# A first projection in three rounded passes, its norm factor moved to the outputs

## The reference, cut to what matters

```python
h = rms_norm(x, g_mix)          # x * rsqrt(mean(x*x) + eps) * g_mix
proj = h @ w_in                 # 2048 -> 4176 + 3360 columns
p_dsa, p_rwkv = proj[..., :DSA_COLS], proj[..., DSA_COLS:]
q, k, v, q_idx, k_idx, w_idx = split_cols(p_dsa, DSA_SPLITS)
y_dsa = dsa_mixer(...)          # indexer picks keys, then softmax attention
p_rwkv = token_shift_mix(p_rwkv, rwkv_shift_mix)   # mixes each token with the one before
y_rwkv = rwkv7_mixer(...)       # a recurrence over tokens, 16 heads of 64
x = x + concat([y_dsa, y_rwkv]) @ w_out
```

## Time and profile before

| | us |
|---|---|
| median of 3 runs | 3308.83 |
| lowest to highest | 3307.78 to 3310.36 |
| the profiled execution's own time | 3304.67 |
| its span, first to last instruction | 3302.9 |
| TensorE busy | 3166.9 (96%) |
| weight loads busy | 2718.0 (82%) |
| VectorE busy | 1857.9 (56%) |
| ScalarE busy | 1396.1 (42%) |
| GpSimd busy | 211.2 (6%) |

### The profile page before, as it was taken

How to read it: one execution, slowest core, us unless ns; L and a number is a source line. 1 busy time by engine, 2 the same in 40 slices (tenths; PEclk the granted TensorE clock), 3 DMA queues, 4 the chain that set the end, 5 groups by cost and what they waited for, 6 DMA issues and landing times.

```text
span 3302.9 us, 46085 instructions
## 1 busy us (share of the span) xinstructions
PE 3166.9 (96%) x18702; PEld 2718.0 (82%) x18702; DVE 1857.9 (56%) x2416; ACT 1396.1 (42%) x1951; POOL 211.2 (6%) x263
## 2 busy tenths in 40 slices
PE   8999999998989999999898899999999999999998
PEld 7777777766768888767797779999998989889896
DVE  3433333356577777767656883444565555545454
ACT  2222222244456666656541013665434434434343
POOL 0000000020000000000137630000000000000000
PEclk9999999998989999999999998999999999999999
DMA  6222222221358888778553333444555555555554
GB/s 239 83 77 77 90 77 79 88 77 67 115 210 325 318 324 315 286 284 308 190 190 119 124 114 123 166 164 178 208 191 179 204 191 185 186 189 183 189 184 148
DMA packets 81782, 581.66 MB, mean 176 GB/s; under 512 B 9009, under 2 KB 9265, under 8 KB 12338
## 3 DMA queue, kind: packets, MB, share of 16 engines
q1 hardware_dynamic: 78912, 566.27, 47.3%
q10 hardware_dynamic: 2674, 12.54, 1.0%
HBM read 574.58 MB, written 4.19 MB: 175 GB/s over the span
## 4 chain that ended last, share of the span: by engine, by line
PE 80%; DVE 11%; DMA 3%; ACT 2%; POOL 2%; issue 1%; SPq 0%; ACTq 0%; DVEq 0%; POOLq 0%
PE PG L784 10%; PE PG L724 8%; PE PG L722 8%; PE PG L725 8%; PE PG L750 5%; PE PG L749 5%; PE PG L748 5%; PE PG L1103 3%; PE PG L1104 3%; PE PG L1105 3%; PE PX L854 3%; DMA ring<-weights 3%; DVE work L2344 2%; DVE ring_r L612 2%; PE PG L693 1%
## 5 line engine op out<-in xcount | busy, mean ns | idle before, releaser
L612 DVE TENSOR_TENSOR ring_r<-ring,work_r 128x1024 fp32r<-128x1024 f32 x532 | 629.9, 1225 | 394.7 <-ACT work_r L605 389.7
L605 ACT ACTIVATE work_r<-ring 128x1024 fp32r<-128x1024 f32 x532 | 534.4, 1052 | 577.5 <-PE PG L725 235.1
L784 PE MATMUL PG<-HT,ring 128*128 128x256 f32 x1728 | 435.1, 389 | 0.0
L612 DVE TENSOR_TENSOR ring_r<-ring,C_r 128x1024 fp32r<-128x1024 f32 x244 | 289.2, 1226 | 222.2 <-ACT C_r L605 218.9
L605 ACT ACTIVATE C_r<-ring 128x1024 fp32r<-128x1024 f32 x244 | 244.9, 1052 | 374.7 <-PE PG L725 255.6
L725 PE MATMUL PG<-work_r,ring_r 128*128 128x256 f32 x1344 | 374.8, 279 | 0.0
L725 PE MATMUL PG<-YT_r,ring_r 128*128 128x256 f32 x1280 | 361.2, 282 | 0.0
L784 PEld LDWEIGHTS PG<-HT,ring 128*128 128x128 f32 x1728 | 311.2, 190 | 55.4 <-issue 10.6
L725 PEld LDWEIGHTS PG<-work_r,ring_r 128*128 128x128 f32 x1344 | 253.3, 188 | 0.0
L749 PE MATMUL PG<-ring_r,HT_r 128*128 128x512 f32 x640 | 252.1, 394 | 0.0
L725 PEld LDWEIGHTS PG<-YT_r,ring_r 128*128 128x128 f32 x1280 | 244.5, 191 | 0.0
(11 more groups left out here) (566 smaller groups left out, 6277.0 us busy)
## 6 DMA issues: line engine op xcount, KB each, us to landing
ring<-weights SPq DMA_DIRECT2D x536, 1024.0 KB, 4.8
XT<-xT SPq DMA_DIRECT2D x4, 512.0 KB, 6.1
XT<-x ACTq DMA_DIRECT2D x1, 2048.0 KB, 9.4
residual<-XT ACTq DMA_DIRECT2D x4, 512.0 KB, 3.0
XT<-residual ACTq DMA_DIRECT2D x1, 2048.0 KB, 10.1
result<-YT SPq DMA_DIRECT2D x8, 256.0 KB, 4.1
C<-constants ACTq DMA_DIRECT2D x1, 1608.0 KB, 9.3
work<-gate_up ACTq DMA_DIRECT2D x1, 1024.0 KB, 13.0
```

Of the source, the lines that this page charges most:

```text
L605: act.activation(w_high(u)[:, c], ring[:, u % RING, c], ACT.Copy).then_inc(w_hi, 1)
L612: dve.tensor_tensor(ring_r[:, u % RING, c], ring[:, u % RING, c], w_high(u)[:, c].bitcast(F32), ALU.subtract).then_inc(w_lo, 1)
L784: mm = pe.matmul(PG[:, u % BANKS, 0:T], ring[:, u % RING, k * P:k * P + P], HT[:, k, :], start=(k == 0), stop=(k == KT - 1))
```

## The change

The first projection is computed in three passes too. Its weights are rounded by half units: `half_high(act, h)` on ScalarE writes half h (0 to 119) into one of four places, and `half_low(eng, h)` subtracts in place, on VectorE for halves 0 to 15 and on GpSimd for the others. `product(u, k)` waits for its half's low part and issues three matmuls. Two halves of one unit are released separately (`half_done`, `unit_done`).

The norm's factor is no longer in the inputs. The inputs are x times `g_mix`, rounded (`HT_r`) and the rest (`XT_r`), so that products can start before the mean square is known. The factor `RS` is applied to the outputs: on r, k, v and misc by VectorE as it takes them from PSUM (`with_factor`), after which ScalarE and VectorE mix them in SBUF; on the first 25 dsa tiles by GpSimd; on the value tiles by ScalarE when it writes them as tokens, with `RS` turned to columns.

In the rounds, ScalarE's halves and VectorE's and GpSimd's further duties are put between the steps by `used_halves`, by the step in which the half four before has been used. "lora" of the next round waits for "var" and no longer for "out"; ScalarE's third eviction waits for "out" in its place. Three late halves come in the index scores, x as tokens is fetched later, and the start fetches vectors, one weight unit and then x. `FILL` and the number of products behind each step are as before.

```diff
@@ filler_ends
-    return upto, [next(f for f in range(len(upto)) if upto[f] >= KT * (q + 1)) for q in range(DSA_PER_PAIR[p])]
+    return upto, [next(f for f in range(len(upto)) if upto[f] >= KT // 2 * (j + 1)) for j in range(total * 2 // KT)]
@@ helpers
+        HALVES = 2 * U0["wo"]
+        FIRST_FILL = 2 * (P1_AT[("v", 0)] + 1)
+        BY_VECTOR = FIRST_FILL + 4
+        def half_high(act, h):
+            u, c = h // 2, slice(h % 2 * (UNIT // 2), (h % 2 + 1) * (UNIT // 2))
+            act.wait_ge(slot_full[u % RING], 16 * (u // RING + 1))
+            if h >= 4:
+                act.wait_ge(unit_done if h % 2 else half_done, u - 1)
+            act.activation(high_half(h), ring[:, u % RING, c], ACT.Copy).then_inc(w_hi, 1)
+        def half_low(eng, h):
+            u, c = h // 2, slice(h % 2 * (UNIT // 2), (h % 2 + 1) * (UNIT // 2))
+            eng.wait_ge(w_hi, h + 1)
+            eng.tensor_tensor(ring_r[:, u % RING, c], ring[:, u % RING, c], high_half(h).bitcast(F32),
+                              ALU.subtract).then_inc(w_lo, 1)
+        def after_half(p, j):
+            h = 2 * (P1_AT[("v", p)] + 1) + j
+            return P1_ORDER[h // 2] if h % 2 else None, h // 2, h + 4
+        def halves_before(p, name, taken, most):
+            ends = filler_ends(p)[1]
+            now = [j for j in range(taken, len(ends)) if name is None or ends[j] < PE_RW.index(name)]
+            return now[:most]
@@ sync
+            sp.dma_start(V[:, :], A["vectors"]).then_inc(s_vec, 16)
+            sp.dma_start(ring[:, 0, :], A["weights"][0]).then_inc(slot_full[0], 16)
             for q in range(4):
-                sp.dma_start(XT[:, 4 * q:4 * q + 4, :], A["xT"][:, 4 * q:4 * q + 4, :]).then_inc(s_x[q], 16)
-            sp.wait_ge(s_x[3], 16)
-            for s in range(RING):
+                sp.dma_start(X0[:, 4 * q:4 * q + 4, :], A["xT"][:, 4 * q:4 * q + 4, :]).then_inc(s_x[q], 16)
+            for s in range(1, RING):
@@ tensor
             def product(u, k):
+                h = 2 * u + k // (KT // 2)
+                if k % (KT // 2) == 0:
+                    pe.wait_ge(w_lo, h + 1)
...
-                mm = pe.matmul(PG[:, u % BANKS, 0:T], ring[:, u % RING, k * P:k * P + P], HT[:, k, :],
-                               start=(k == 0), stop=(k == KT - 1))
+                pe.matmul(o, wh, HT_r[:, k, :], start=(k == 0), stop=False, skip_group_check=True)
+                pe.matmul(o, wh, XT_r[:, k, :], start=False, stop=False, skip_group_check=True)
+                mm = pe.matmul(o, wl, HT_r[:, k, :], start=False, stop=(k == KT - 1), skip_group_check=True)
+                if k == KT // 2 - 1:
+                    mm.then_inc(half_done, 1)
...
-                    pe.wait_ge(DR.sem, DR.at(p - 1, "out"))
+                    pe.wait_ge(DR.sem, DR.at(p - 1, "var"))
@@ scalar, pair(p)
+                def used_halves(before, most=1):
+                    for j in halves_before(p, before, taken_[0], most):
+                        taken_[0] += 1
+                        what, u, h = after_half(p, j)
+                        if what and what[0] == "dsa":
+                            act.wait_ge(unit_done, u + 1)
+                            act.activation(DQ[:, what[1], :], PG[:, u % BANKS, 0:T], ACT.Copy) \
+                               .then_inc(free_bank(u), 1)
+                        if h < 2 * V_UNIT + 3:
+                            half_high(act, h)
@@ scalar, attention
                 act.wait_ge(DR.sem, DR.at(MT - 1, "out"))
+                half_high(act, 2 * V_UNIT + 3)
+                act.wait_ge(a_cos, 25)
...
                 for q in range(3):
+                    half_high(act, 2 * (V_UNIT + 2 + q))
+                    half_high(act, 2 * (V_UNIT + 2 + q) + 1)
                     take_v(q)
@@ vector
+            def with_factor(what):
+                m, u = MIX_ORDER.index(what), P1_AT[what]
+                dve.wait_ge(unit_done, u + 1)
+                dve.tensor_tensor(MBF[:, m % 3, 1:T + 1], PG[:, u % BANKS, 0:T], RS[:, :], ALU.mult) \
+                   .then_inc(free_bank(u), 1)
+            def mix(what, dst):
+                m, c = MIX_ORDER.index(what), MU_COL[what]
+                dve.wait_ge(s_mixed, m + 1)
+                return dve.scalar_tensor_tensor(dst, MBF[:, m % 3, 1:T + 1], ONEMU[:, c:c + 1], dst, ALU.mult, ALU.add)
@@ gpsimd
+            for p in range(MT):
+                for j in range(len(filler_ends(p)[1])):
+                    what, u, h = after_half(p, j)
+                    if what and what[0] == "dsa" and what[1] < 25:
+                        pool.wait_ge(free_bank(u), u // BANKS + 1)
+                        pool.tensor_tensor(DQ[:, what[1], :], DQ[:, what[1], :], RS[:, :], ALU.mult).then_inc(a_cos, 1)
+                    if h == BY_VECTOR:
+                        pool.wait_ge(w_lo, BY_VECTOR)
+                    half_low(pool, h)
+            late = dict(zip((7, 11, 15, 19, 22), range(2 * V_UNIT + 4, HALVES)))
             for r in range(25):
+                if r in late:
+                    half_low(pool, late[r])
```

More of the change, by code:

```diff
@@ L285, in build @@
         V = sb("V", [P, NV])
-        SQ = sb("SQ", [P, 4, T])
         RS = sb("RS", [P, T])
@@ L683, in _, with unit @@
         def _(pe):
-            def unit(u, use, x, kts=KT, tiles=1, first=None, full=0, free=0):
+            def unit(u, use, x, kts=KT, tiles=1, full=0, free=0):
                 pe.wait_ge(slot_full[u % RING], 16 * (u // RING + 1) + full)
@@ L690, in unit @@
                     for k in range(kts):
-                        if first is not None and t == 0:
-                            pe.wait_ge(s_h, first + k + 1)
                         last = pe.matmul(PG[:, (use + t // 2) % BANKS, (t % 2) * T:(t % 2) * T + T],
@@ L796, in pair @@
                 for w in "rkv" if p == 0 else "":
-                    unit(P1_AT[(w, p)], P1_AT[(w, p)], HT)
+                    products(P1_AT[(w, p)])
                 step = iter(range(len(PE_RW)))
@@ L1409, in pair @@
                 taken_ = [0]
-                _, ends = filler_ends(p)
-                def take_dsa(before):
-                    while taken_[0] < len(ends) and ends[taken_[0]] < PE_RW.index(before):
-                        d = sum(DSA_PER_PAIR[:p]) + taken_[0]
-                        u = P1_AT[("dsa", d)]
-                        act.wait_ge(unit_done, u + 1)
-                        act.activation(DQ[:, d, :], PG[:, u % BANKS, 0:T], ACT.Copy).then_inc(free_bank(u), 1)
-                        taken_[0] += 1
+                def used_halves(before, most=1):
+                    for j in halves_before(p, before, taken_[0], most):
+                        taken_[0] += 1
+                        what, u, h = after_half(p, j)
[4 more added lines that the diff above has]
+                        if h < 2 * V_UNIT + 3:
+                            half_high(act, h)
                 def done(ins, name):
                     ins.then_inc(AR_.sem, AR_.step(p, name))
-                for w in "rkv":
-                    mix((w, p))
+                mix(("r", p), R_)
+                mix(("k", p), K_)
+                mix(("v", p), V_)
                 if p == 0:
+                    half_high(act, FIRST_FILL + 3)
                     act.wait_ge(s_vprep, 4)
@@ L1889, in _ @@
             dve.tensor_scalar(LO[0:32, 2, :], LO[0:32, 2, :], 0.5, 0.5, ALU.mult, ALU.add).then_inc(s_lo_dve, 1)
+            for h in range(10, FIRST_FILL + 3):
+                half_low(dve, h)
+                if h >= 10 and h % 2:
+                    with_factor(("rkv"[(h - 11) // 2], 0)) if h < FIRST_FILL + 3 else None
+            with_factor(("v", 0))
             def pair(p):
@@ L1899, in me, with used_halves @@
                     dve.wait_ge(DR.sem, DR.at(p, name))
+                taken_ = [0]
+                def used_halves(before):
+                    for j in halves_before(p, before, taken_[0], 2 * KT):
+                        taken_[0] += 1
+                        what, u, h = after_half(p, j)
+                        if what and what[0] != "dsa":
+                            with_factor(what)
                 mix(("r", p), R_)
                 mix(("k", p), K_)
-                mix(("v", p), V_)
-                v = P1_AT[("v", p)]
-                dve.wait_ge(free_bank(v), v // BANKS + 1)
+                link(mix(("v", p), V_))
+                if p == 0:
+                    half_low(dve, FIRST_FILL + 3)
                 done(dve.memset(ZB[:, 0, :], 0.0), "k")
@@ L1915, in pair @@
                 done(dve.tensor_tensor(CP, CS, EW, ALU.subtract), "cum")
+                used_halves("kks")
                 pe("kks")
@@ L2520, in _ @@
                                    ALU.mult).then_inc(a_cos, 1)
+            for h in range(HALVES - 3, HALVES):
+                half_low(pool, h)
             for q in range(4):
```

233 lines of the change are left out of this document (138 added, 95 removed).

## The result

The changed kernel is slower: 3355.97 us median (3352.92 to 3362.32, 4 runs) against 3309.60 beside it (3307.78 to 3314.17), ratio 1.0141, 95% interval 1.0122 to 1.0159. The forecast was 3317, its range ended at 3334. The profiled execution took 3362.32 us, its span is 3360.5, 57.6 longer than before.

What follows compares the result with a forecast made beforehand. Looked bound by TensorE, but shorter fills gain only where longer than other engines' turns. Start -11.5, pairs -5, clock +4, rope +21 gave +8.5 on 3304.67: 3313, median 3317; range 3284 to 3334, the forecast's own 3304 to 3330.

Steps and rivals of the forecast that it cites:

- Price of a product: First projection: a product costs 0.351 us in three passes instead of 0.431; 960 products take at most 77 us off.
- The start, -11.5: Before the first pair: first product at about 10.8, first pair at 50.5 against 62.0; bounds -14 and -7.
- The pairs, -5: Recurrence's eight pairs: front loses 0.5 us, rest gains 1.1, net -0.6 a pair; ends -32 and +12.
- the clock, +4: Pairs: TensorE gaps of 2 to 3 us lower the granted clock, costing 0.5 us a pair; bounds 0 and +14.
- with a 0.6 us collision with GpSimd's scaling of a finished DSA tile, tilde is done at 614.4: Front of a pair, VectorE's chain to the tilde operands: done at 614.4 instead of 612.74, tok starts at 614.5.
- The collision at the output: Pair front: GpSimd's half after the Exp, 599.4 to about 602.1, delays the three mixes; step k done at 603.6.
- The masks: Pair, after tok: five masks wait for GpSimd's half until about 622.2; square step at 625.4 instead of 624.89.
- port rarely hit: Rival, pairs: mixes escape GpSimd's halves, each pair gains 4 us; total -22, 3286; chance 0.34.
- collisions feed on each other: Rival, pairs: masks and mixes lose 1.5 us a pair more, clock stays low through square steps; 3335; chance 0.14.
- The rope part, +24.3 and -3.7: Attention: GpSimd's five low halves lengthen it by 24.3 us, 46 cheaper products return 3.7; net +20.6, bounds +12 and +26.
- At nothing: Put at zero: ScalarE's kks-fill halves, GpSimd's DSA scaling, later x tokens, stages behind; below 10 us together if covers go.
- the one addition behind GpSimd: Pairs' chunk loop: one addition behind GpSimd, subtracted with two evictions behind a ScalarE half, leaving 1.1 us gained a pair.

Runs made afterwards that it cites:

- e4: Changed kernel plus 54 matmuls without use per pair on TensorE, ahead of its waits for kks and tok; 3359.7 us, ratio 1.0165.
- e3: Changed kernel with the pairs' low halves left out (8 of 1024 columns subtracted, third matmul reads the high half); 3312.0 us, ratio 1.0010.
- e2: Changed kernel with all low halves of the pairs on VectorE, at places where it waits, none on GpSimd; 3316.3 us, ratio 1.0013.
- e1: Changed kernel plus one GpSimd wait per pair: scaling and low halves after the kks fill wait for the tilde products; 3353.7 us, ratio 1.0148.
- e10: e1 plus one wait: GpSimd's three halves behind the rope part wait for the last rope sum; 3347.9 us, ratio 1.0130.
- e6: Changed kernel with GpSimd's late halves ahead of rope steps 12, 16, 20, 24 instead of 7, 11, 15, 19, 22; 3374.9 us, ratio 1.0218.
- e11: Changed kernel with late halves only at rope steps 12, 16, 20, the other five waiting for the last rope sum; 3366.5 us, ratio 1.0187.
- e12: e2 with the edits of e11, and the three halves inside the rope part on VectorE instead of GpSimd; 3297.4 us, ratio 0.9980.

## Why the prediction was wrong, point by point

- **Price of a product.** Right. 0.12 from matmul to matmul at the full clock, 0.351 forecast for three; TensorE's busy time in the pairs fell.
- **The start, -11.5.** Measured -11.1. The path differed: ScalarE loads a table first (1.28 us at 7.10), and the first product also waits for x's low part, which VectorE makes behind two halves of weights, so it came at 12.47 instead of 10.8. That the time comes out so close is in part luck: the products behind it must have lost less than I had allowed.
- **The pairs, -5, and the clock, +4.** Together -1 forecast, +40.9 measured: 42 of the 49 us by which the profiled execution misses the forecast (of the rest, 9 arose behind attention). The step that failed is "with a 0.6 us collision with GpSimd's scaling of a finished DSA tile, tilde is done at 614.4". I had the lock, its length and the queue right, but placed both halves of the kks fill behind tok. With shorter products TensorE has used both of the halves that must be free before ScalarE is through with its exponentials (the second one's last product starts at 308.36); ScalarE then rounds two halves at once, and GpSimd takes them while VectorE is at the products. What stood at 0.6 is 4.9 us: 0.55 for the scaling, as forecast, and 2.17 + 2.14 for the two halves, which stood at nothing in that place. The collision at the output was sized right in effect: the step k ends 4.4 us after the output's product begins, forecast 4.5, though the output and not the mixes was hit (mixes 0.474, median). The masks, which I had expected to be hit, were not (0.69): the third half was over before them.
- **The clock's term** came out at 2.3 us a pair by e4, 18 in all: not the 0.5 a pair that I took, and beyond the upper bound of 14. I had the wait before tok at 2 to 3 us, and it is 4.45; that the term follows the length of the wait is my reading, no run varied it alone.
- **The rival "port rarely hit"**: its gain of 4 us a pair is what e3 shows (76.8 to 72.5) and e2 nearly reaches. The bound was right, its condition did not hold: four products a pair are hit.
- **The rival "collisions feed on each other"** named the direction, but for the masks and the mixes, which were not hit, and with 1.5 us a pair where there were 5. Its 3335 adds 22 us to the profiled execution's 3313; on the median it is 3339.
- **The rope part, +24.3 and -3.7.** Measured +21.3, and +18.7 to the end of attention, against +20.6. Step 7's sum comes 33.7 us after the last output, forecast 34.6, behind a wait of 12.09, forecast about 12; a step with a half in it loses 2.1 more.
- **At nothing**: e3 keeps ScalarE's halves and GpSimd's scaling of the DSA tiles, and its pairs are 4 us shorter than before, so these two covers held, but for the 0.55 of the scaling above. In the chunk loop the one addition behind GpSimd, which I had counted, is there: the last z addition took 2.15 instead of 0.29. The stages behind attention, put at nothing too, are 9.1 longer in the profiled execution; why is open.

What stays open: what exactly in the index part lets the clock stay or fall, and why the pairs of one and the same code had a clock of 0.97 in e1's profile and 0.94 in e10's. That GpSimd's halves, not ScalarE's, cost the pairs their time is shown (e1, e2, e3); that an even denser entry would hold the clock always is not.

## What to carry to other kernels

A cheap engine that shares a port is placed by time, not by load: ask for each of its long instructions which instruction of the other engine begins beside it *after* the change has moved everything, and whether it lies on the path. A collision ahead of a TensorE stage is paid as a wait and again as the clock behind it. And where a gain upstream is not seen in the total, compare the granted clock of the stages behind it: here 68 us won in the pairs came out as 34 in the median of e2 (46 above the kernel before, then 12), since six of its ten runs have the lower clock.

## Unexpected on the hardware

- GpSimd's 128x1024 subtraction (2.34 to 2.54 us) held back VectorE instructions of two SBUF operands (0.42 to 2.59), and a tensor_scalar of one (0.30 to 2.48), but not a reciprocal beside it (1.70 at 302.42), nor one that reads PSUM: all 16 copies from PSUM in the inverse (L2067) took 0.69, and eight of them began beside a half. In the changed kernel GpSimd's instruction was itself never slowed by more than 0.2.
- The index part runs at either of TensorE's two clock levels for nearly all of its length, with the same code and TensorE recorded as busy throughout: 33 us in the changed kernel, 57 to 58 in e6 and e11. The Trainium skill, "TensorE: Matmul & The Clock Gate", Part 1, lets sustained matmul work lift the clock to its full level. If work recorded as busy is what it means, the trace does not agree here: 50 us of it at 0.50 in e12.
